# Two buffers of tap matrices instead of three, and repeated tokens moved within the expert slots

## The reference

```python
def block(args):            # 128 tokens; it: 128 expert numbers of each token; gt: their gates
    xt, it, gt = args
    u = expert_u[it]
    v = expert_v[it]
    act = jax.nn.gelu(jnp.einsum("td,ted->te", xt, u), approximate=False)
    return jnp.einsum("te,ted->td", gt * act, v)
```

```python
a, b, g = jnp.split(h @ w_in, 3, axis=-1)
y = a * jax.nn.sigmoid(b)
y = lax.conv_general_dilated(y, dw[:, None, :], ...)   # each channel by itself, 31 taps
```

## Time and profile before

| what | us |
|---|---|
| median of three runs | 1192.42 |
| lowest and highest run | 1188.33, 1192.83 |
| the profiled execution's own time | 1192.42 |
| its span from the first to the last instruction | 1190.6 |
| PE busy | 925.2 |
| DVE busy | 790.1 |
| ACT busy | 338.5 |
| POOL busy | 323.6 |

### The profile page before, as it was taken

The page is one execution under the profiler, slowest core; times in us unless marked ns, Lnnn a source line. Parts: engine busy times, 40 slices in busy tenths (PEclk is TensorE's granted clock), DMA queues, the critical chain, the costliest instruction groups (busy, mean ns, idle before and its releaser), DMA issues. The chain is left out here.

```text
span 1190.6 us, 19278 instructions
## 1 busy us (share of the span) xinstructions
PE 925.2 (78%) x7592; PEld 742.0 (62%) x7592; DVE 790.1 (66%) x2085; ACT 338.5 (28%) x816; POOL 323.6 (27%) x284
## 2 busy tenths in 40 slices
PE   7999999877786895967244548987675459999998
PEld 6899688865674682755011216875463239978887
DVE  5665646697897767755488887777765658933411
ACT  2511111145222223121011133566551215233100
POOL 0001000232253333523254444454454400000000
PEclk9899999998897897887556568998886659999999
DMA  9987695799999999999999999999999966313100
GB/s 371 380 322 303 251 406 220 307 424 423 403 414 423 393 424 421 424 421 422 424 420 420 421 420 420 417 417 420 419 417 421 415 262 234 142 71 107 71 1 36
DMA packets 51563, 402.62 MB, mean 338 GB/s; under 512 B 5649, under 2 KB 7953, under 8 KB 9105
## 3 DMA queue, kind: packets, MB, share of 16 engines
q0 software_dynamic: 40320, 293.62, 60.0%
q1 hardware_dynamic: 10288, 105.62, 22.1%
q10 hardware_dynamic: 864, 2.16, 0.5%
HBM read 400.32 MB, written 1.05 MB: 337 GB/s over the span
## 5 line engine op out<-in xcount | busy, mean ns | idle before, releaser
L456 POOL DMA_INDIRECT arena<-uv_dram,arena x192 | 231.3, 1204 | 343.6 <-PE ps L627 273.7
L1627 DVE CUSTOM_DVE_ANT_0 arena<-arena 128x1024 f32<-128x1024 f32 x192 | 233.1, 1224 | 95.2 <-DMA arena<-uv_dram,arena 85.3
L627 PE MATMUL ps<-arena 128*32 128x256 f32 x1536 | 138.9, 493 | 172.3 <-DVE arena L1654 172.1
L627 PEld LDWEIGHTS ps<-arena 128*32 128x32 f32 x1536 | 47.8, 130 | 235.4 <-DVE arena L1654 194.8
L1146 ACT ACTIVATE gel<-dots 128x2 f32<-128x2 f32 x128 | 26.0, 203 | 411.4 <-DVE dots L1627 378.4
L510 PE MATMUL ps<-xn,wring 128*128 128x128 f32 x896 | 110.0, 284 | 4.3 <-DMA wring<-units_dram 2.3
L510 PEld LDWEIGHTS ps<-xn,wring 128*128 128x128 f32 x896 | 106.4, 199 | 11.0 <-issue 6.1
L456 POOL DMA_INDIRECT wring<-uv_dram,arena x64 | 79.2, 1238 | 109.9 <-PE ps L627 99.9
L1627 DVE CUSTOM_DVE_ANT_0 wring<-wring,arena 128x1024 f32<-128x1024 f32 x64 | 77.8, 1224 | 41.0 <-DMA wring<-uv_dram,arena 39.1
L627 PE MATMUL ps<-wring,arena 128*32 128x256 f32 x512 | 44.3, 476 | 60.7 <-DVE arena L1654 59.5
L1654 DVE TENSOR_SCALAR arena<-const,gel,arena 128x32 f32<-128x32 f32 x256 | 64.7, 304 | 18.8 <-ACT gel L1146 14.2
(11 more groups left out here) (288 smaller groups left out, 1489.5 us busy)
## 6 DMA issues: line engine op xcount, KB each, us to landing
wring<-units_dram SPq DMA_DIRECT2D x39, 2048.0 KB, 10.0
arena<-mod_dram POOLq DMA_DIRECT2D x24, 1024.0 KB, 9.8
arena<-units_dram SPq DMA_DIRECT2D x8, 2048.0 KB, 8.6
arena<-uv_dram,arena POOLq DMA_INDIRECT x192
wring<-units_dram SPq DMA_DIRECT2D x2, 1024.0 KB, 6.3
hA<-x_t_dram SPq DMA_DIRECT2D x2, 512.0 KB, 7.1
arena<-mem_t_dram SPq DMA_DIRECT2D x1, 1024.0 KB, 9.7
arena<-keys_dram ACTq DMA_DIRECT2D x2, 512.0 KB
```

Of the source, the lines that this page charges most:

```text
L456: pool.indirect_dma_start(ring[b], None, uv_d, bass.IndirectOffsetOnAxis(ap=idx[:, n:n + 1], axis=0)).then_inc(sem(f"row_in{b}"), 16)
L627: mm = pe.matmul(acc_ps(q)[G * c:G * (c + 1), :], lhsT=diag[:, s % 2, j, :], rhs=ring[b][:, D + 256 * c:D + 256 * (c + 1)], start=(p == 0 ...
L1627: post(V.tensor_tensor_reduce(out=ring[b][:, 0:D], in0=ring[b][:, 0:D], in1=x_rep[q % 2], scale=1.0, scalar=0.0, op0=ALU.mult, op1=ALU.add ...
```

## The change

It has three parts.

1. `tap_chunk` has two buffers instead of three. ACT waits, ahead of writing chunk `c`, for PE's chunk `c - 2` instead of `c - 3`.
2. PE writes the repeated tokens at `p` = 10 and 12 instead of 10 and 13, and does it at the end of the slot, behind `gate_products` and `conv_chunk`, instead of directly behind line 627.
3. ACT copies them at `p` = 11 and 13 instead of 12 and 15.

```diff
-
-        tap_chunk.append(ypad[:, :, 15 + P:15 + S])
@@ conv_chunk
-                    mm = pe.matmul(tile_ps(f"cv{b}")[:, 0:CUT], lhsT=tap_chunk[c % 3][:, i], rhs=ypad[:, b, tap:tap + CUT],
+                    mm = pe.matmul(tile_ps(f"cv{b}")[:, 0:CUT], lhsT=tap_chunk[c % 2][:, i], rhs=ypad[:, b, tap:tap + CUT],
@@ slot of PE
-                if p in (10, 13) and q + 1 < GROUPS:
-                    if p == 10 and (q == 0 or q + 1 == GROUPS // 2):
-                        need(pe, "xn", 12 if q else 7)
-                    repeated_tokens(q + 1, (p - 10) // 3)
                 if q in H3_GROUPS and p in (5, 6):
                     h3_sums(H3_GROUPS.index(q), p - 5)
                 if 0 <= s - AB_SLOT < 2 * KB:
                     gate_products((s - AB_SLOT) // 2, (s - AB_SLOT) % 2)
                 if 0 <= s - CONV_SLOT < KB * CHUNKS:
                     conv_chunk(s - CONV_SLOT)
+                if p in (10, 12) and q + 1 < GROUPS:
+                    if p == 10 and (q == 0 or q + 1 == GROUPS // 2):
+                        need(pe, "xn", 12 if q else 7)
+                    repeated_tokens(q + 1, p // 2 - 5)
@@ diagonals
-                if c >= 3:
-                    used = c - 3
+                if c >= 2:
+                    used = c - 2
@@ slot of ACT
-                if p in (12, 15) and q + 1 < GROUPS:
-                    repeated_tokens(q + 1, p // 3 - 4)
+                if p in (11, 13) and q + 1 < GROUPS:
+                    repeated_tokens(q + 1, p // 2 - 5)
```

More of the change, by code:

```diff
@@ L1111, in diagonals @@
                 for i, tap in enumerate(taps):
-                    ins = act.activation(tap_chunk[c % 3][:, i], ident, ACT.Copy, scale=col("cv_dw", 8 * tap + b))
+                    ins = act.activation(tap_chunk[c % 2][:, i], ident, ACT.Copy, scale=col("cv_dw", 8 * tap + b))
                 post(ins, "tap_diag")
```

## The result

| | before | changed kernel |
|---|---|---|
| median of 20 runs each, us | 1190.64 | 1196.96 |
| lowest and highest run, us | 1187.21, 1196.62 | 1192.34, 1201.88 |
| the profiled execution's own time, us | 1192.42 | 1200.94 |
| its span, us | 1190.6 | 1199.1 |

The ratio is 1.0052, with a 95% interval of 1.0038 to 1.0066. The changed kernel is 6.3 us slower (4.5 to 7.9). The forecast was 2.5 us more.

The account below looks back on a forecast made before the run. Gathers were taken to bound the convolution slots and PE the rest. 2 us for slots 90 to 93, 0.5 for slots 106 to 109 and 0 elsewhere gave 2.5 us on 1192.42: 1195 us, range 1188 to 1204.

Parts of the forecast that it names:

- the cover: Queued gathers in the convolution slots hide a stall's first 9 us, chosen between 7.4 and 12.1 us.
- The bound: Convolution slots, 740 to 902 us: bound by gathers, DMA share 1.01 at 418 GB/s; the rest bound by PE.
- First pair, how late: Group 5, slots 90 to 93: slot 91 5.0 us late, slot 93 11 us; 2 us lost, bounds 0 to 4.2.
- Second pair: Group 6, slots 106 to 109: slot 107 3.8 us late, slot 109 6.5 to 8; price 0.5 us (0 to 1).
- Group 4: Slots 74 to 77, first gate products between line 627 and the tokens: about 2.5 us late, covered.
- Two buffers: Tap matrices in two buffers: two-slot loop of 9.1 us fits two slots at 5.0 us each; price 0.
- Groups 0 to 3: Beside the second tile's chain: copy holds the gelu about 1 us in each of 8 slots; price 0, bounds -1 to +2.
- Size of the copies' waits: Slots 91, 93, 107 and 109: ACT's copy waits 1 to 3 us each for PE's repeated tokens.
- The other signs: DVE waits several us for gelu; POOL's issues for slots 95, 97 5 and 10 us late; DMA digits stay 9.
- Thinner cover: Rival, convolution slots: queued gathers hide only 4.6 us, costing 10.4 us, 1203 us in all; chance 0.22.
- Buffers bind too: Rival: recovery fails between slots 93 and 107, both stall pairs add up, plus 3 us from the loop, 1205 us; chance 0.08.
- faster: Rival: earlier gate products, chunks and tokens help where DMA lacks work in groups 0 to 3; 1189 us; chance 0.10.

Follow-up runs that it names:

- the first stall alone: The changed kernel with ACT's copies of the tokens at p = 11 and 15 instead of 11 and 13; 1192.06 us against 1189.81, ratio 1.0014.
- with three buffers: The changed kernel with the third tap_chunk buffer put back, so only the repeated tokens are moved on PE and ACT; 1196.92 us, ratio 1.0057.
- the kernel with groups 4 to 6: The kernel before, three buffers, with the repeated tokens in the new places on PE and ACT in groups 4, 5 and 6 only; 1194.88 us, ratio 1.0042.
- the long hold: The kernel before, with ACT writing the chunk of slot 95 nine times instead of once, ahead of the gelu; 1201.97 us, ratio 1.0109.
- the five kernels that lose nothing: The kernel before, and those with two buffers alone, either move put back, or only groups 0 to 3 moved; slots 90 to 127 took 186.3 to 186.4 us.

## Why the prediction was right in kind and short in size

The direction, the place and the mechanism held, and the measured median lies in the range given, 1188 to 1204. The sum (2 + 0.5 + 0 = 2.5 us) was short of the measured 6.3. That lies outside the "0 to 5 us more" that had a chance of 0.60, and at the edge of "slower by over 0.5%", which had 0.30. The step that failed is the cover, taken as 9 us.

- **The bound.** Gathers bind the slots. Confirmed by the first stall alone: 7.3 us of lateness, 0.4 us of loss. (All of slices 8 to 31 in the earlier trace rows lie at 393 to 424 GB/s; there are no two or three exceptions, as the prediction had it.)
- **First pair, how late.** Worked out 5.0 us for slot 91 and 11 for slot 93 (9.0 at full clock, 11.6 at half). The trace has 5.2 and 11.1. The half clock behind the idle time, taken from the earlier trace rows, came as there, and added 0.9 + 1.1 = 2.0 us in slot 91 (1.94 for 1.07, 3.17 for 2.05) where 2.6 were worked out.
- **The cover: the term that was mis-sized.** 9 us were taken, from a choice between 7.4 and 12.1; 6.2 were measured, below the lower bound. The first pair then costs 11.1 - 6.2 = 4.9 by the sum and 5.8 in the trace, and not 2. The bound of 12.1, which pulled the choice up from 7.4, has a gather that takes its own 2.5 us alone, and 9 us ask for one that has landed 14.6 - 9 = 5.6 us behind its issue. The next section has what the gathers took behind the stall: 6.4 to 8.0 us in the changed kernel. By these the same subtraction gives 6.6 to 8.2 us, so that the bound of 7.4, from the first gather's 7.2, was near and the 9 was not. Why the changed kernel's own 5.3 lies below even 6.6 is not shown. "Bounds" of 0 to 4.2 us for this pair were too narrow for the same reason.
- **Second pair.** Worked out 3.8 us late at slot 107, 6.5 to 8 at slot 109, price 0.5 (0 to 1). The trace has 4.4 and 8.0 beyond the 5.8 of slot 106, so the upper end of the lateness was the true one, and it costs 7.6 - 5.8 = 1.8 us here, 1.7 with three buffers, and 0.4 in the kernel with groups 4 to 6. With a cover of 6.2 the 8.0 give 1.8.
- **Group 4.** Worked out 2.5 us late, covered. The copies waited 5.45 and 7.22 us there, slots 75 and 77 were 1.7 and 2.1 us late, and slot 80 was not late any more. Covered.
- **Two buffers.** 0, confirmed by a ratio of 1.0013 (0.9996 to 1.0029) and by an unchanged stretch. (Ten slots, 82 to 91, have both gate products and a chunk, and not eight; the 0 does not hang on it.)
- **Groups 0 to 3.** 0, with bounds of -1 and +2, which the timed runs do not narrow; the traces show nothing beyond their scatter of 2.5 us.
- **Size of the copies' waits.** "1 to 3 us each" in the last part was wrong: 7.83, 8.19, 7.11 and 6.02 us. ACT is free for the copy when the gelu before it ends, and waits for the whole of PE's slot. The lateness had been worked out from PE's rows, and so did not depend on it.
- **The other signs.** Two of them held: DVE's wait for the gelu (29.4 us), and POOL's issues for slots 95 and 97, 5.6 and 11.5 us late. Those that hung on the cover failed: the DMA digits fell to 8, the last gather was issued 7.7 us later (963.69 against 952.30, less the 3.7 of slot 90) and not 2, and a sign of "wrong" came, slice 27 at 354 GB/s. The waits of line 1110 for line 611, another such sign, came too (16.0 us, the longest 2.7), and the kernel with two buffers alone has them without loss.
- **The rivals.** "Thinner cover" was the nearest in kind: 4.6 us and +10.4 were forecast, 6.2 us of cover in the mean and +6.3 came. Its condition was a cover below about 6 us, and the mean stands just above it, the changed kernel's own 5.3 below. Its argument, that one lagging engine sets the landing, is borne out by the landing signals in the next section, but the thicker cover that the prediction drew from slow engines did not come. "Buffers bind too" is excluded by the two kernels that have one part alone, "faster" by the interval.

In the profiled pair slots 90 to 127 explain +7.6 us and the timed runs have +6.3 (4.5 to 7.9). The two agree within the interval. Whether the tail gives back some of it is open: its length varied by up to 4.6 us between kernels that have the same tail.

## What to carry to other kernels

Ahead of a duty that is moved, write down what now stands between two engines' streams: if A waits for the end of B's slot and B's next slot waits for A, the slot grows to the sum of both, however idle A is. Either move alone (last in PE's slot, or early on ACT) left the stretch as it was, 186.3 us, and the pair cost 6 us. And a queue of transfers is a threshold, not a price per stall: size it with a hold of known length put into the kernel, since the time from issue to use (14.6 us) overstated it by more than a factor of two, and read the effect from the stretch of slots rather than from the span.

## What the runs showed of the hardware

**The time from issue to use is transfer in hand only for the part of a gather that lands last.** In the changed kernel the last gather was again 14.59 us in the chain, as in the earlier trace rows:

```profile
963.69 14.59 DMA wring<-uv_dram,arena
980.16 1.98 PE ps L625 x16
```

Eight buffers at 2.5 us go round in 20 us, so this number only says that use and release take the other 5.4 us. In the long hold the last gathers were issued by 806.1 us and the transfers all but stood still from 815 us on: the DMA engines taken together had about 9 us of work behind an issue, and the hold lost the bytes of 15.7 us (the five rows against 421 GB/s) while the slot came 17.7 us late. So, in the mean of the DMA engines, only 2.0 us of the stall were covered by work in hand. The other 4.6 us, 15.7 less the 11.1 that reached the end, were caught up later at the same 421 GB/s. The changed kernel has the same shape: 11.1 us late, 9.6 us of bytes lost, 5.8 us at slot 106, so 1.5 and 3.8.

What is caught up at an unchanged rate can only be a distance between what is moved and what is used. The packets' own times in the traces show it (the 8 KB packets counted in order of their ends, 256 to a slot): in the kernel before, the mean packet of a slot's pair of gathers was done 5.5 us ahead of the dots at slot 94, and 3.1 us ahead in the changed kernel at slot 100, behind the stall. This lead does not come back. At slot 126 it is 4.9 to 5.6 us in the five kernels that lose nothing and 1.3 to 1.8 us in all eight others, also in the one with the first stall only, whose stretch is 0.4 us longer.

Where the lead comes from stands in the landings. A gather adds 16 signals to its semaphore in the trace, as many as there are DMA engines, and they do not come together. The trace of the kernel before lacks some of these signals; the kernel with two buffers alone has all of them and runs these slots as before. Mean times behind the issue, us, each rounded by itself:

| | slots | first signal | last signal | between them |
|---|---|---|---|---|
| two buffers alone, no stall | 84 to 90 | 7.1 | 14.2 | 7.0 |
| | 116 to 127 | 7.1 | 14.6 | 7.6 |
| the changed kernel | 84 to 90 | 7.7 | 13.8 | 6.1 |
| | 100 to 105, behind the first pair | 10.7 | 13.7 | 3.0 |
| | 116 to 127, behind the second | 12.1 | 14.2 | 2.1 |

In undisturbed slots the part of a gather that comes last lands at its use (first gather of slot 94: last signal and use 14.0 us behind the issue) and sets the pace, while the first parts have been done for 7 us. At a stall the others run dry first, and bytes are lost while the last part still has work: in the long hold 15 signals of the last gather ahead of it had come by 816.9 us, and the last came at 820.4. Behind the stall all parts stand nearly together. The second pair shows the other side of it. With the parts together, a further 8.0 us of lateness lost the bytes of only 3.2 us (869 to 909 us, against 421 GB/s), where the first pair lost those of 9.6 in 11.1. The cover was about the same, 5.3 and 6.2 us.

The Trainium skill, "DMA: Bandwidth & Descriptors", section "Latency and other measured facts", names two DMA engines that are usually slower on this path. The trace agrees in that some parts of every gather lag. It does not say which engines they are, and not why.

**A gather with little queue ahead of it** was as quick as the first one. In the changed kernel the six gathers of slots 95 to 97, issued from 799.57 to 816.63 us, had all 16 signals 6.4 to 8.0 us behind their issue; their use came 10.1 to 17.9 us behind it, since DVE was held by the gelu. So the time from issue to use is no measure of a gather there, and the first gather's 7.2 us were a fair one. In three other kernels one gather, the first of slot 96, had landed after 5.4 to 5.6 us, between others that took 7.7 to 8.1. The Trainium skill's fixed 2.0 us plus bytes at 436 GB/s ("DMA: Bandwidth & Descriptors", section "Anatomy of one DMA"), 4.4 us by estimate for this gather, is less than any of these, and would have made the cover 10.2 us, further off than the value taken.

**The clock behind idle time.** After 4.93, 4.11 and 19.23 us of idle the next 16 records of PE took 1.94, 1.94 and 1.93 us instead of 1.07. In the changed kernel's row from 815 to 820 us the granted clock was 0.55, near the lower of its two levels (1.2 GHz), and in the row from 820 to 825 us 1.00 again, the upper (2.4 GHz). It added to the lateness of the second slot of a pair, as the prediction had it.
